# The router multiplies rows not yet normed, and the output product is cut in two halves with router, ranks and turns between them

## What is computed

```python
def rmsnorm(x, g):
    xf = x.astype(jnp.float32)
    y = xf * lax.rsqrt(jnp.mean(xf * xf, axis=-1, keepdims=True) + EPS)
    return (y * g.astype(jnp.float32)).astype(x.dtype)

def token_mixer(...):
    ...
    merged = jax.nn.sigmoid(z_ga) * attn + jax.nn.sigmoid(z_gb) * sgu
    return x + merged @ w_o, c_kv, k_rope, v

def channel_mixer(x, norm2_g, w_rg, b_rg, w_re, b_re, w_gate, w_up, w_down):
    xt = rmsnorm(x, norm2_g).reshape(b * s, d)
    g_logit = (xt @ w_rg).astype(jnp.float32) + b_rg.astype(jnp.float32)
    g_w, g_idx = lax.top_k(jax.nn.softmax(g_logit, axis=-1), 1)
    e_logit = ((xt @ w_re) + b_re).reshape(b * s, N_GROUPS, EXPERTS_PER_GROUP)
    ...                                   # of the best group the two best experts
    y = grouped_expert_ffn(xt, expert, weights, w_gate, w_up, w_down)
    return x + y.reshape(b, s, d)
```

## Time and profile before

| | us |
|---|---|
| median of 3 runs | 2010.71 |
| lowest and highest of them | 2010.27, 2015.7 |
| the profiled execution, its own time | 2013.47 |
| its span, first to last instruction | 2011.7 |
| this stage in it | about 1230 to 1426 |
| the experts in it, from the first rows turned to the end of their products | 1445 to 1968 |

### The profile page before, as it was taken

The page is one execution under the profiler, slowest core; times in us unless marked ns, Lnnn a source line. Parts: engine busy times, 40 slices in busy tenths (PEclk is TensorE's granted clock), DMA queues, the critical chain, the costliest instruction groups (busy, mean ns, idle before and its releaser), DMA issues. The chain is left out here.

```text
span 2011.7 us, 28826 instructions
## 1 busy us (share of the span) xinstructions
PE 1827.2 (91%) x11390; PEld 1243.5 (62%) x11390; DVE 736.0 (37%) x1659; ACT 451.8 (22%) x998; POOL 306.8 (15%) x428
## 2 busy tenths in 40 slices
PE   7999999988899999999999997999598888988894
PEld 5678888877765656656666664555365555555551
DVE  2343333445423334334555554555322211111116
ACT  3122122111113323222334433222110111101103
POOL 1022211121100000000111112243412111111100
PEclk9999999999999999988999998999698989988997
DMA  7112222487630000025999995444599999999986
GB/s 207 55 65 80 80 75 77 137 306 259 229 109 1 1 0 1 1 63 163 280 296 291 305 296 217 154 182 162 193 410 420 419 416 417 412 401 404 412 352 261
DMA packets 105004, 432.93 MB, mean 215 GB/s; under 512 B 24192, under 2 KB 29792, under 8 KB 74112
## 3 DMA queue, kind: packets, MB, share of 16 engines
q1 hardware_dynamic: 84608, 330.01, 43.9%
q0 software_dynamic: 20160, 101.24, 15.1%
q10 hardware_dynamic: 128, 0.20, 0.0%
HBM read 388.17 MB, written 63.66 MB: 225 GB/s over the span
## 5 line engine op out<-in xcount | busy, mean ns | idle before, releaser
L908 PE MATMUL psum<-arena 128*128 128x256 f32 x1792 | 403.1, 384 | 20.6 <-DVE arena L2105 6.4
L908 PEld LDWEIGHTS psum<-arena 128*128 128x128 f32 x1792 | 340.7, 192 | 77.2 <-DVE arena L2083 7.6
L1377 PE MATMUL psum<-arena 128*64 128x256 f32 (+1 forms) x2048 | 287.2, 415 | 59.9 <-DMA arena<-in_w_up_dram 59.7
L1377 PEld LDWEIGHTS psum<-arena 128*64 128x64 f32 (+1 forms) x2048 | 203.4, 156 | 133.8 <-issue 78.9
L1135 PEld LDWEIGHTS psum<-arena 128*128 128x128 f32 x1024 | 115.5, 143 | 29.3 <-issue 27.8
L1396 PE MATMUL psum<-arena 128*64 128x512 f32 (+1 forms) x512 | 131.4, 595 | 1.5 <-DVE arena L2425 0.8
L2421 DVE TENSOR_TENSOR arena<-arena,psum 128x256 f32<-128x256 f32 x36 | 15.2, 422 | 317.6 <-ACT arena L1677 317.6
L1135 PE MATMUL psum<-arena 128*128 128x128 f32 x1024 | 129.2, 280 | 0.0
L1265 PE MATMUL psum<-arena 128*128 128x512 f32 x256 | 114.6, 605 | 1.3 <-ACT arena L1612 1.3
L1577 ACT COPY arena<-psum 128x512 f32<-128x512 f32 x128 | 71.9, 587 | 175.4 <-PE psum L1135 175.4
L1891 POOL DMA_INDIRECT y_rows<-arena x36 | 40.6, 1128 | 409.4 <-DVE arena L2430 387.8
(11 more groups left out here) (328 smaller groups left out, 2176.3 us busy)
## 6 DMA issues: line engine op xcount, KB each, us to landing
arena<-in_w_gate_dram SPq DMA_DIRECT2D x64, 1024.0 KB, 12.6
arena<-in_w_up_dram SPq DMA_DIRECT2D x64, 1024.0 KB, 19.8
arena<-in_w_down_dram SPq DMA_DIRECT2D x64, 1024.0 KB, 21.6
arena<-in_w_in_dram SPq DMA_DIRECT2D x8, 2048.0 KB, 9.3
z_act<-arena SPq DMA_DIRECT2D x64, 256.0 KB, 2.0
rope_turned<-arena SPq DMA_DIRECT2D x32, 512.0 KB, 4.8
arena<-rope_turned SPq DMA_DIRECT2D x64, 256.0 KB, 9.9
arena<-z_act SPq DMA_DIRECT2D x8, 2048.0 KB, 10.2
```

What stands on the lines that cost most here:

```text
L908: last = mm(out[:, 0:256], x[:, k, :], w[:, k, :], start=(k == 0), stop=(k == 3))
L1377: last = mm(bank(2 + u)[rows, DE * x:DE * x + DE], xg_t[u][:, k, rows], w_e[slot][x][:, k, :], start=(k == 0), stop=(k == KD - 1))
```

## The change

The router no longer waits for the norm. The rows are turned as `add_x` left them (`turn_x2` reads `xr`), the gain of the norm is multiplied into the router's weights once, early on POOL, and the root, a factor of each row, is applied when the logits are taken from PSUM (`take_logits` becomes a scalar_tensor_tensor with `stat5`). `norm2` is cut into `root2` (the reciprocal) and `norm2` (the normed rows, which the experts still need). The ranks go to banks 7, 0, 1 and 5 instead of 4 and 5.

The order changes on PE, DVE and ACT, and SP waits for one thing more.

```diff
+RANK_BANK = (7,) * (NTP - 2) + (0, 1, 5)
...
                 sp.dma_start(bs_t, b_s[0].rearrange("g i -> i g")).then_inc(small_in, 16)
+                sp.dma_start(g2_t, norm2_g[0].rearrange("(k p) -> p k", p=P)).then_inc(small_in, 16)
...
                 sp.wait_ge(o_n, n + 1)
                 sp.wait_ge(x2_cp, n + 1)
+                sp.wait_ge(ot_mm, n + 1)
                 x_again(n + 2)
...
             def out_product(n, r=P, halves=(0, 1)):
                 pe.wait_ge(mt_ev, n + 1)
-                if n >= 3:
-                    pe.wait_ge(r_pos, n - 2)
+                if n:
+                    pe.wait_ge(x2_ok, n)
...
-            def turn_normed(n, s, r=P):
-                pe.wait_ge(o_n, n + 1)
+            def turn_x2(n, r=P):
+                pe.wait_ge(x2_ok, n + 1)
                 pe.wait_ge(lg_ok, n + 1)
+                if n >= 2:
+                    pe.wait_ge(r_pos, min(n - 1, 6))
...
             def ranks(t):
                 pe.wait_ge(r_dve, t + 1)
-                pe.wait_ge(x2_ok, min(t + 3, NT))
...
+            pe.wait_ge(wr_ok, 1)
             for n in range(1, NTP):
...
-                turn_normed(n - 1, 1 - s)
-                out_product(n)
-                turn_merged(n + 1, 1 - s, rows_of(n + 1))
+                turn_x2(n - 1)
+                out_product(n, halves=(0,))
                 router(n - 1)
                 if n >= 2:
                     ranks(n - 2)
-            turn_normed(7, 1)
+                turn_merged(n + 1, (n + 1) % 2, rows_of(n + 1))
+                out_product(n, halves=(1,))
+            ranks(6)
+            turn_x2(7)
             out_product(8, RS)
             router(7)
-            ranks(6)
-            turn_normed(8, 0, RS)
+            turn_x2(8, RS)
+            ranks(7)
             router(8, RS)
-            ranks(7)
...
                     v_stat(n + 2, s % 2, i + 2 if s == 1 else i + 3)
+                    act.wait_ge(y_mm, n + 1)
+                    merged_t(n + 1)
                     x2_stat(n, s % 2)
-                    merged_t(n + 1)
...
+            pool.wait_ge(small_in, 16 * (10 + NB))
+            for k in range(KD):
+                last = G.tensor_scalar(w_router[:, k, :], w_router[:, k, :], g2_t[:, k:k + 1], None, ALU.mult)
+            last.then_inc(wr_ok, 1)
...
-            def take_logits(n, lg_rows, r=P):
+            def take_logits(n, s, r=P):
                 dve.wait_ge(lg_mm, n + 1)
-                tt(lg_rows, bank(6)[0:r, 0:72], rbias[0:r, :], ALU.add).then_inc(lg_ok, 1)
+                dve.wait_ge(o_inv, n + 1)
+                stt(logits[0:r, n, :], bank(6)[0:r, 0:72], stat5[s][0:r, 3:4], rbias[0:r, :], ALU.mult, ALU.add).then_inc(lg_ok, 1)
...
-                add_x(n, u, n // 2 + 1, r)
-                take_logits(n - 1, logits[:, n - 1, :])
-                norm2(n, u, n // 2, r)
+                take_logits(n - 1, 1 - u)
                 if n >= 2:
                     positions(n - 2)
                 choose(n - 1)
-            take_logits(8, logits[0:RS, NTP, :], RS)
+                add_x(n, u, n // 2 + 1)
+                root2(n, u)
+                norm2(n, u, n // 2)
+            positions(6)
+            add_x(8, 0, 5, RS)
+            take_logits(7, 1)
+            choose(7)
+            root2(8, 0, RS)
+            positions(7)
+            take_logits(8, 0, RS)
             stage_end(dve, 4)


-            positions(7)
             choose(8)
+            norm2(8, 0, 4, RS)
             positions(8)
```

More of the change, by code:

```diff
@@ L286, in build @@
         page_raw = take(NCH).bitcast(I32)
+        g2_t = take(KD)
         x2_at = [SIZE - NT * D]
@@ L1273, in out_product @@
                     last.then_inc(y_mm, 1)
-            def turn_normed(n, s, r=P):
-                pe.wait_ge(o_n, n + 1)
+            def turn_x2(n, r=P):
+                pe.wait_ge(x2_ok, n + 1)
                 pe.wait_ge(lg_ok, n + 1)
+                if n >= 2:
+                    pe.wait_ge(r_pos, min(n - 1, 6))
                 for k in range(KD):
-                    last = tr(bank(6, 2)[:, P * k:P * k + r], normed_rows(n)[0:r, P * k:P * k + P], ident[0:r, 0:r])
+                    last = tr(bank(6, 2)[:, P * k:P * k + r], xr[n % 2][0:r, P * k:P * k + P], ident[0:r, 0:r])
                 last.then_inc(ot_mm, 1)
@@ L1303, in ranks @@
                 pe.wait_ge(r_dve, t + 1)
-                pe.wait_ge(x2_ok, min(t + 3, NT))
-                if t == 7:
-                    pe.wait_ge(r_pos, t)
-                out = bank(4 if t < NTP else 5)[:, 0:NE]
+                out = bank(RANK_BANK[t])[:, 0:NE]
                 last = mm(out, const("before"), mask[t % 2], start=True, stop=(t == 0))
@@ L1311, in ranks @@
                 last.then_inc(r_pe, 1)
+            pe.wait_ge(wr_ok, 1)
             for n in range(1, NTP):
-                s = n % 2
-                mix(n + 1, 1 - s)
+                mix(n + 1, (n + 1) % 2)
                 if n == 1:
@@ L1532, in _ @@
                     turned_setup(t - 5)
-            act.wait_ge(p_sq, 1)
-            A(stat, stat, ACT.Sqrt, bias=eps).then_inc(p_rs, 1)
+            act.wait_ge(stat_in, 2)
+            A(stat, stat, ACT.Sqrt, bias=eps).then_inc(stat_out, 1)
             def z_slot(m):
@@ L1657, in _ @@
                     last.then_inc(mt_ev, 1)
+                if n + 1 < NT:
+                    act.wait_ge(y_mm, n + 1)
+                    merged_t(n + 1, rows_of(n + 1))
                 x2_stat(n, n % 2, rows_of(n))
-                if n + 1 < NT:
-                    merged_t(n + 1, rows_of(n + 1))
+            normed_t(8, RS)
             act.wait_ge(o_n, NT)
             act.dma_start(xt_rows[NTP * P:TOK, :], xo[0][0:RS, :]).then_inc(xt_st[0], 16)
-            normed_t(8, RS)
             stage_end(act, 4)
@@ L1702, in _ @@
                         expert_out(NST + j, 0, yo_used + 1 + j)
-            act.wait_ge(r_sub, 1)
+            act.wait_ge(stat_in, 3)
             A(g_exp, g_sub, ACT.Exp)
-            A(d_exp, d_sub, ACT.Exp).then_inc(r_exp, 1)
+            A(d_exp, d_sub, ACT.Exp).then_inc(stat_out, 1)
             a_step = Count(act, act_c)
@@ L1739, in _ @@
             step(G.tensor_copy(page_idx, page_raw))
-            G.tensor_scalar(page_int, page_idx, 8.0, const("p_mod"), ALU.mult, ALU.add).then_inc(idx_ready, 1)
+            step(G.tensor_scalar(page_int, page_idx, 8.0, const("p_mod"), ALU.mult, ALU.add))
             pool.wait_ge(z_ev, 2 * NT)
@@ L1991, in _ @@
                     combine_x(t // 2)
-            dve.sem_inc(p_sq, 1)
-            dve.wait_ge(p_rs, 1)
+            dve.sem_inc(stat_in, 1)
+            dve.wait_ge(stat_out, 1)
             step(V.reciprocal(rstd, stat))
@@ L2285, in choose @@
                 lg = logits[:, t, :]
+                dve.wait_ge(lg_ok, t + 2)
                 step(V.max(g_top[:, t, :], lg[:, 0:NG]))
@@ L2310, in positions @@
                 dve.wait_ge(r_pe, t + 1)
-                step(tt(prod, hot[t % 2], bank(4 if t < NTP else 5)[:, 0:NE].unsqueeze(1).broadcast_to([P, 2, NE]), ALU.mult))
+                step(tt(prod, hot[t % 2], bank(RANK_BANK[t])[:, 0:NE].unsqueeze(1).broadcast_to([P, 2, NE]), ALU.mult))
                 step(red(rk[:, t, :], prod, AX.X, ALU.add))
@@ L2327, in _ @@
             dve.wait_ge(uv_in, 48)
+            root2(0, 0)
             norm2(0, 0, 0)
-            for n in range(1, NT):
-                u, r = n % 2, rows_of(n)
+            for n in range(1, NTP):
+                u = n % 2
                 if n + 1 < NT:
```

34 lines of the change are left out of this document (17 added, 17 removed).

## The result

| | us |
|---|---|
| before, median of 4 runs (2010.27 to 2015.7) | 2011.68 |
| changed kernel, median of 4 runs (2034.75 to 2045.79) | 2038.79 |
| ratio, 95% interval | 1.0125 (1.0103 to 1.0147) |
| the changed kernel's profiled execution, and its span | 2041.51, 2039.7 |

The change made the kernel 1.25% slower. The forecast was 2033.1 with a range of 2024 to 2041. Within the two profiled executions the difference is 28.0 us, and this is where it lies. The parts are measured between marks inside each stage, because the stages before this one vary by some us from one execution to the next.

What follows compares the result with a forecast made beforehand. PE, busy 98.00 of 98.00 us, bounds the regular turns, with a nearly as long load chain that the change lengthens. +28.6 - 0.8 - 5.4 = +22.4 gives 2035.9 profiled, 2033.1 for the median, range 2024 to 2041.

Steps and rivals of the forecast that it cites:

- the ring through the load: Output-product stage: norm2, z_load, v_stat, v_norm, logits, positions, choose, add_x sum to 23.63 us against PE's turn of 19.47.
- the signs: Regular turns: PE busy about four fifths, waiting about 5 us; add_x right behind choose; z_load about 5.1 after add_x.
- the rival with the clock: PE's clock falls after its waits, costing 3 to 6 us in the last turn and end: about 2037, chance 0.12.
- The regular turn, 24.5: add_x to add_x in turns with a load: 23.63 plus 0.9 of POOL's hold, 24.5 against 19.47.
- POOL's hold, 0.9: POOL's gate multiplication holds the third operation of positions on DVE, 0.7 of the 1.27 left: 0.9 per turn.
- The first turn, +5.0: SP's new wait for turn_x2(0) delays z_load(3) to 1268.67, so add_x(1) comes 5.0 us later.
- The last turn, -0.8: Turn from add_x(6) to add_x(7), with no load to wait for: 18.9 against 19.70, -0.8.
- The end of the stage, -5.4: From add_x(7) to ranks(8): 21.4 instead of 26.8, a gain of 5.4 reaching the end in full.
- MoE weights loaded ahead: Experts' weight loads at the stage's end: issued some 1 us later relative to the end, over 10 us spare, costing nothing.
- the 2035.9 that the sum gives: Whole run: the terms' sum of +22.4 added to the profiled execution's 2013.5.
- The rival "loads hidden after all", 2007.5: z rows arrive 5.8 us sooner, PE stays full and the gains stand: 2007.5, chance 0.07.

Runs made afterwards that it cites:

- experiment 1: Changed kernel with SP issuing z_load(n+3) before the wait for norm2(n+1) instead of behind it: 2011.86, ratio 1.0002.
- experiment 2: Kernel before the change, with the same earlier z_load on SP: 2012.92, ratio 0.999.
- experiment 3: Changed kernel with DVE's logits, positions and choose moved in front of v_norm: 2032.64, ratio 1.0105.
- experiment 5: POOL's drain removed: early z_load kernel 2013.37, kernel before 2014.46. Early z_load with ACT's stage end before its norm2(8) wait: without drain 2018.51, with drain 2013.79.
- experiment 6: Early z_load kernel plus norm2(8) ahead of positions(7), 2011.75; plus last 4 MB of weights held until the slot table landed, 2013.25; plus both, 2012.95.
- e6: Early z_load kernel without POOL's drain and with ACT ending the stage before its wait for norm2(8): 2018.51, ratio 1.0021.

## Why the prediction was right, point by point

**Direction and mechanism: right.** The regular turns are no longer set by PE but by the ring through the load. add_x waits for choose, PE for add_x, the clock fell. Experiments 1 and 2 show it from both sides. Of the signs, z_load left 5.13 after add_x as forecast, and add_x stood right behind choose. PE was busy 0.86 of the time and not four fifths, and waited for add_x 2.04, 4.65, 2.24, 4.13 and 4.08 us and not about 5: the half products behind those waits took up to 8.7 and not 7.04, and filled part of the idle time. The measured 2038.8 lies nearest to the 2037 of the rival with the clock, but that is by chance, as the last turn and the end below show.

**The regular turn, 24.5: right in the mean.** Measured were 24.12, 24.32, 25.52 and 25.15, a mean of 24.78, and 22.16 for the last one with a load (22.9), whose load took 7.65 and not 8.6. In the first two a shorter load than the 10.2 of the earlier trace rows, 9.55 and 9.76, makes up for a longer hold by POOL (next point), which is luck. In the two long turns it took 10.93 and 10.58, so that the four loads have the forecast mean. There POOL issues two scatters some us ahead of it; that they lengthen it was not tested.

**POOL's hold, 0.9: too small.** It was 1.32, the whole remaining time of the multiplication. This is the result of the Trainium skill's page "SBUF — State Buffer", section "Who interferes with whom": a DVE instruction with two SBUF inputs and a GpSimd one exclude each other for the whole instruction, which gave an estimate of 1.27 here. The trace agrees with it, by 1.32 against 1.27. In experiment 3 an operation of 128x8 with a single SBUF tensor input was held too, by 2.17. Not every small operation is held: beside L1838 in the turn shown, the logits and the first step of positions, with an input in PSUM, took 0.28 and 0.27, and the reduction behind them (L2327) 0.29, as without POOL. By the rule v_norm in the earlier trace rows would have ended at 1298.67 + 1.29 = 1299.96; it ended at 1299.75. I had made a factor of 0.7 out of this fifth of a us, and the small operation was held in full.

**The first turn, +5.0: right.** z_load(3) left 8.69 after add_x(0) and not 5.31, so 3.4 later (forecast 3.3), and the turn was 26.65 against 21.54, +5.1. With the load early it is still 24.15: there the router (1.90) and the turn of the merged rows (1.04) stand ahead of the product's end, 2.6 of them on the path.

**The last turn, -0.8: -0.55,** 19.15 against 19.70. Both half products ran in 7.04 and 7.14, at a granted clock of 1.00, since PE had not waited before them. The rival in which the clock costs 3 to 6 more did not come about. Where PE had waited, the half product took 8.61 as above, but PE had to wait for choose anyway.

**The end of the stage, -5.4: the term that failed.** From add_x(7) to ranks(8) the gain was even larger, 26.82 to 19.66; 1.1 of that is product(8), which took 4.00 at a granted clock of 1.00 and had taken 5.08 at 0.71. But I let it reach the end in full, and forecast that past ranks(8) every row would keep its distance. The 15.95 to the first gather became 21.84. The largest part, 3.5, is POOL's, as divided in experiment 5: the forecast followed DVE and PE to ranks(8) and never POOL, whose drain, scatters and memset had been hidden behind DVE. For the weights my step said "MoE weights loaded ahead are issued some 1 us later relative to the end and have over 10 us", and asked only whether the weights were in time, not what they would delay. norm2(8) moved behind choose(8); tile 8's store went out at add_x(7) + 21.1 instead of + 16.5, and the weights behind it at + 23.5 instead of + 22.3, while the table read had moved 2.7 the other way. In experiments 5 and 6, with the drain away, the weights held or norm2(8) first, the first product came only 0.4 to 1.1 sooner. Of 7.2 us 1.3 were left, where the forecast had 5.4. This, +4.1, is most of the 5.6 between the 2035.9 that the sum gives for the profiled execution and the 2041.5 measured. The turns make 0.7 more, and the parts ahead of the stage and behind the first gather, -1.3 and +2.1, are about what executions of the same code differ by.

**The rival "loads hidden after all", 2007.5:** its condition was made true in experiment 1, and the time was 2011.9. The rival lay 3.2 below the kernel before, and the run, by its ratio, 0.4 above it, with an interval of some 3 us either way. The end's gain, which was in its sum too, makes 3.7 of this: the first expert product came 1.7 sooner after add_x(7) and not 5.4. The turns cost 2.3 in all, against the 2.2 in its sum.

## What to carry over

Before small operations are moved out of the shadow of a transfer, draw the ring that the transfer belongs to and ask which wait lets it start: here the cure was one wait on SP's queue, not another order of the work. A gain at the end of a stage has to be followed through every queue to the next stage's first product, DMAs issued ahead "for free" included; they delay whatever small read the end hangs on. And a small DVE operation of a kind that POOL holds (here those with two inputs in SBUF, and the tensor_scalar) is to be costed as the whole remaining time of POOL's operation beside it.

## What the runs showed that I had not expected

- A DVE operation of 128x8 takes 2.34 us instead of 0.17 while POOL multiplies 128x1024. The price is set by POOL's operation, not by the size of one's own. POOL's memset, which reads nothing, did the same in e6.
- A 64 KB read takes 2.2 us with the DMA engines at 30 GB/s, 3.7 us at 241 (changed kernel, 1459.70 to 1463.30), and 5.1 us at 302, with 4 MB of weights under way.
- Holding those weights back moves the wait and does not remove it: the gather after it goes from 3.50 to 7.96 us.
